# Dilated heads in 64x64 score blocks: one turning for two heads, fewer stores, later loads, and a head of attention in another order

## The chip, the cores and the metric

The kernel runs on one core of one Trainium2 chip. The metric is the device time of one execution in microseconds, smaller is better. Three runs of the kernel before gave a median of 2364.34 us (2364.12 to 2364.73).

## The reference, cut to what matters

Two layers. Each normalises x, projects it to q, k and v, mixes tokens in three groups of heads, projects back, and adds a SwiGLU feed-forward part. All arithmetic is float32. The change touches group C, six heads of dilated attention. Each head attends in three branches, with dilation 1, 4 and 16 (in the code: `mid` tiles, `c2` and `c3`), and the branches are merged by their softmax denominators.

```python
DIL_BRANCHES = ((128, 1), (512, 4), (2048, 16))

def dilated_attention(q, k, v, slopes):
    b, h, s, hd = q.shape
    outs, lses = [], []
    for window, d in DIL_BRANCHES:
        L = s // d                     # 1024, 256, 64
        def to_sub(t):                 # every d-th token: d subsequences of L tokens
            return t.reshape(b, h, L, d, hd).transpose(0, 3, 1, 2, 4).reshape(b * d, h, L, hd)
        o, lse = banded_attention(to_sub(q)[:, :, None], to_sub(k), to_sub(v),
                                  window // (2 * d), slopes[:, None], d)
        ...
    w = jax.nn.softmax(jnp.stack(lses), axis=0)
    o = jnp.einsum("nbhs,nbhsd->bhsd", w, jnp.stack(outs).astype(jnp.float32))
```

With dilation 16 a subsequence (a remainder of the position by 16) has 64 tokens, and each of its tokens attends to those 64. With dilation 4 it has 256 tokens, and a block of 128 queries needs 192 keys.

## The kernel before

**Stages of a layer.** Values and 14 units of 128 q/k columns are projected (`half_unit`, 24 matmuls per half unit), normalised over each head by ACT (`qk_square`, `qk_rms`, `qk_variance`) and DVE (`square_low`, `qk_finish`), then come attention, the output projection and the feed-forward part. Outside attention every product is three matmuls 512 columns wide.

**Tiles and steps of attention.** A tile is one head against one block of 128 queries. `tiles` has 48 tiles of kind `c3` (dilation 16), 48 of `c2` (dilation 4), and 128 of the banded kinds `b0`, `mid`, `b7`. Four tiles make a step: steps 0 to 11 score `c3`, 12 to 23 `c2`, 24 to 55 the rest. Six dilated tiles (the six heads) make a group `gi`, 0 to 15, a step and a half each. In a step k, `pe_step(k)` does in this order

- the scores of tiles 4k to 4k+3 (`score_pair`, two pairs),
- the products with the values of tiles 4k-8 to 4k-5 (`weigh`),
- the turning of the weights of tiles 4k-4 to 4k-1 (`unit`: transposes into PSUM).

DVE adds the distance table to the scores and takes the minimum (`tmin`), ACT takes the exponential (`exponential`), and the turned weights are copied from PSUM to `PT` by DVE or ACT (`copy_unit`; DVE's copy is the last thing in its step, and with one row of a step DVE has it). `weigh` in step k+1 waits for the copies of step k (`copied`). Tile n keeps its weights in `T[:, n % 8, :]`.

**c3 before.** One tile takes two remainders at once: 128 queries against 128 keys. The two 64x64 blocks off the diagonal are masked out by the table (1e34). A tile has one turning of 128 columns, `weigh` does two matmuls for it, one for each 64 queries. **c2 before.** 128 queries against 192 keys, two turnings (the second one of columns 128 to 255, its last 64 unused), four matmuls in `weigh`. A step of four tiles turns 4 blocks of 128 columns in `c3`, 8 in `c2`; they lie in one or two rows of up to 512 columns, each copied by one instruction.

**POOL.** `stage(gi)` gathers queries and keys of group gi from `QK` into `QS`, `KS` (two buffers; it waits until group gi-2 is scored, and `score_pair` waits for it). Between the stages POOL clears parts of `VC` (gi 4) and `VR` (gi 5), takes the power of the last unit's variances (gi 7, `POWERED`), and multiplies that unit by the roots (`scale_last(0)`, `scale_last(1)`, gi 12 and 13), which step 24 needs (`qk_s`). After stage 15 it makes the 12 tables of the grid heads (`bias_table`), which step 27 needs.

**SP's one queue.** For each gi, in order: `store_group(gi)` (waits until ACT has put the group away, `grp_s`), perhaps `spread_roots` (the variances go out to DRAM and come back transposed, their roots go out and come back broadcast to 64 partitions; its last step writes `RM_LAST`, which `scale_last` waits for), `load_values(gi + 4)`, then other loads for later: `MASK`, `BIAS`, `VC` (`load_neighbours`), `VA` (`load_grid`). After gi 15 come the stored groups of the first banded block (`g_back`), which `branch_min(0)` on DVE waits for in step 27.

**The head of attention.** The score of tile 0 comes after the last product of unit 13. DVE does tile 0's `tmin` and then `square_low(13, 1)`. ACT does `qk_square(13, 1)`, `qk_variance(26)`, `keep_raw(0)` and then the first exponential; in step 1 also `qk_variance(27)` and `keep_raw(1)`.

```python
                sp.wait_ge(stat, 2 * QT)          # before the first load_values
...
                    elif gi in (12, 13):
                        scale_last(gi - 12)
...
                for gi in range(C_GROUPS):
                    store_group(gi)
                    if gi in SPREAD_AT:
                        spread_roots(SPREAD_AT[gi])
                    if gi + 4 < C_GROUPS:
                        load_values(gi + 4)
```

## Time and profile before

| what | value |
|---|---|
| median of 3 runs | 2364.34 us |
| profiled execution, its own time | 2367.3 us |
| its span, first to last instruction | 2365.8 us |
| mean granted TensorE clock | 0.996 of full |
| busy share of the span: PE, DVE, ACT, POOL | 99%, 67%, 45%, 28% |
| steps 0 to 24 of attention, layer 0 | 255.88 to 316.60 us |
| the same, layer 1 | 1430.35 to 1490.97 us |

The span is cut in engines' busy times, in stretches, and in single instructions with the idle time ahead of them and what ended it. A float32 matmul of attention appears as two records (8 records are 4 matmuls), a transpose as one. A record's length includes its way through the array, so records overlap; the price of one more is the distance between starts, not the length. The last half unit of the projection and the two dilated kinds together take some 61 us in each layer.

### The profile page before, as it was taken

The numbers are of one execution on the slowest core, as the hardware profiler recorded it, in microseconds if no ns is written. First come the engines' busy times: TensorE is split into PE (matmuls) and PEld (weight loads), VectorE is DVE, ScalarE is ACT, GpSimd is POOL, SyncE is SP. The second block draws the span as 40 slices with busy tenths as digits, with TensorE's granted clock in tenths as the row PEclk, the third lists the DMA queues.
The fourth block names the chain that finished last, engine by engine and source line by source line (L and its number), as shares of the span: only waits on it lengthen the run. The fifth ranks groups of instructions, "written<-read, shape, count | busy, mean of one in ns | idle before, by whom it ended". The sixth has DMA issues, their size and how long they took to land. (4 is left out here: it accounts for less than half of the span.)

```text
span 2365.8 us, 38274 instructions
## 1 busy us (share of the span) xinstructions
PE 2330.3 (99%) x14504; PEld 1933.6 (82%) x14504; DVE 1592.7 (67%) x2871; ACT 1073.1 (45%) x2048; POOL 656.5 (28%) x571
## 2 busy tenths in 40 slices
PE   9999999999999999999999999999999999999998
PEld 9988777787888888888898887777878888888887
DVE  5389778737555555789844897787475555557897
ACT  4333778735223222444533338786452222324434
POOL 1000456411544444100010005553124444441000
PEclk9999999999999999999999999999999999999999
DMA  6231341231222211721352214303322222218222
GB/s 236 68 58 53 88 123 30 76 135 66 91 84 80 87 57 54 292 77 63 111 187 57 55 44 133 86 23 122 107 71 81 81 80 81 58 49 311 71 81 98
DMA packets 233986, 225.19 MB, mean 95 GB/s; under 512 B 50260, under 2 KB 192084, under 8 KB 233816
## 3 DMA queue, kind: packets, MB, share of 16 engines
q1 hardware_dynamic: 233816, 222.89, 29.5%
q8 instruction: 110, 1.80, 0.3%
q14 instruction: 60, 0.49, 0.1%
HBM read 171.00 MB, written 53.41 MB: 95 GB/s over the span
## 5 line engine op out<-in xcount | busy, mean ns | idle before, releaser
L1810 DVE TENSOR_TENSOR WL<-RAW,WH 128x512 fp32r<-128x512 f32 x132 | 160.5, 1217 | 151.3 <-ACT WH L1276 151.3
L2506 PE MATMUL psum<-ABH 128*128 128x512 f32 x616 | 240.1, 390 | 1.1 <-DVE X L1896 1.1
L2507 PE MATMUL psum<-ABL,ABH 128*128 128x512 f32 x616 | 239.7, 389 | 0.0
L2508 PE MATMUL psum<-ABH,ABL 128*128 128x512 f32 x616 | 239.7, 389 | 0.0
L2472 PE MATMUL psum<-HL,WH 128*128 128x512 f32 x704 | 217.4, 390 | 0.7 <-DVE HL L1816 0.7
L2472 PE MATMUL psum<-OPH_t,WH 128*128 128x512 f32 x528 | 207.1, 392 | 5.9 <-DVE U L1831 5.9
L2472 PE MATMUL psum<-OPL_t,WH 128*128 128x512 f32 x528 | 207.1, 392 | 1.0 <-DVE OPH_t L1816 1.0
L1810 DVE TENSOR_TENSOR WL<-WS,WH 128x512 fp32r<-128x512 f32 x172 | 138.5, 806 | 84.2 <-ACT WH L1276 84.2
L2151 POOL TENSOR_TENSOR WS<-RAW 128x512 f32<-128x512 f32 x84 | 143.3, 1706 | 130.6 <-DMA x_res<-X 130.6
L2183 PE MATMUL psum<-HH,UH 128*128 128x512 f32 x448 | 174.6, 390 | 1.3 <-ACT VB L1050 1.3
L2184 PE MATMUL psum<-HL,UH 128*128 128x512 f32 x448 | 174.3, 389 | 0.0
L2185 PE MATMUL psum<-HH,UL 128*128 128x512 f32 x448 | 174.3, 389 | 0.0
L1500 DVE RECIPROCAL RM<-RM 128x512 f32<-128x512 f32 x52 | 174.0, 3345 | 0.0
L1126 ACT ACTIVATE T<-T,G 128x192 f32<-128x192 f32 (+3 forms) x352 | 154.0, 468 | 28.8 <-DVE G L1547 26.6
L2472 PEld LDWEIGHTS psum<-HL,WH 128*128 128x128 f32 x704 | 131.7, 188 | 29.2 <-DVE HL L1816 1.5
L2048 POOL COPY QS<-QK 128x384 f32<-128x384 f32 x32 | 30.2, 943 | 443.6 <-DVE QK L1503 255.8
L2183 PE MATMUL psum<-PH,HH 128*128 128x512 f32 (+1 forms) x384 | 143.7, 374 | 0.0
L2185 PE MATMUL psum<-PH,HL 128*128 128x512 f32 (+1 forms) x384 | 142.6, 371 | 0.0
L2184 PE MATMUL psum<-PL,HH 128*128 128x512 f32 (+1 forms) x384 | 142.5, 371 | 0.0
L2472 PE MATMUL psum<-OPH_t,WL 128*128 128x512 f32 x352 | 138.2, 393 | 0.0
L2506 PEld LDWEIGHTS psum<-ABH 128*128 128x128 f32 x616 | 115.6, 188 | 26.8 <-DVE X L1896 2.0
L2472 PE MATMUL psum<-OPH_b,WH 128*128 128x512 f32 x352 | 137.1, 390 | 0.0
(262 smaller groups left out, 5587.7 us busy)
## 6 DMA issues: line engine op xcount, KB each, us to landing
RAW<-in_w_gu SPq DMA_DIRECT2D x176, 256.0 KB, 3.9
WDS<-in_w_down SPq DMA_DIRECT2D x88, 256.0 KB, 2.5
UR<-in_w_in SPq DMA_DIRECT2D x56, 256.0 KB, 3.3
g_mid<-GRES SPq DMA_DIRECT2D x28, 512.0 KB, 2.6
WDK<-in_w_down SPq DMA_DIRECT2D x44, 256.0 KB, 5.9
x_res<-X SPq DMA_DIRECT2D x2, 4096.0 KB, 13.0
PR<-in_w_out SPq DMA_DIRECT2D x32, 256.0 KB, 4.8
X<-x_res SPq DMA_DIRECT2D x2, 4096.0 KB, 13.0
```

What stands on the lines that cost most here:

```text
L1126: a.activation(T[:, n % 8, off:off + w], T[:, n % 8, off:off + w], ACT.Exp, scale=-1.0, bias=G[:, 6 * V1 + place_:6 * V1 + place_ + 1]).th ...
L1500: v.reciprocal(RM[:, hf, :], RM[:, hf, :]).then_inc(rec_s, 1)
L1810: v.tensor_tensor(WL[SLOT[i, j]][:, :, :], w_source(i, j), WH[SLOT[i, j]][:, :, :].bitcast(F32), ALU.subtract).then_inc(w_lo, 1)
L2048: g.tensor_copy(dst, dilated_rows(bd, T_CQ, q, P)).then_inc(staged, 1)
L2151: g.tensor_tensor(to[i][:, :, :], first, second, op).then_inc(w_sum, 1)
L2183: t.matmul(dst, sh, mh, start=start, stop=False)
L2184: t.matmul(dst, sh, ml, start=False, stop=False)
L2185: return t.matmul(dst, sl, mh, start=False, stop=stop)
L2472: last = t.matmul(dst[:, :], w[SLOT[i, j]][:, k, :], h[o][:, k, :], start=(i in (1, 5, 6) and k == 0 and part == 0), stop=(i in (2, 3, 4) ...
L2506: t.matmul(dst, ah, bh, start=open_, stop=False, skip_group_check=True)
L2507: t.matmul(dst, ah, bl, start=False, stop=False, skip_group_check=True)
L2508: last = t.matmul(dst, al, bh, start=False, stop=shut, skip_group_check=True)
```

## The change

1. **c3 scores.** `score_pair` does two 64x64 matmuls per tile instead of one of 128x128: each half of the output partitions holds one remainder's 64 keys. Scores, table, `tmin` and exponential are 64 columns wide. The two heads of a pair write their weights side by side in `T` (`weights_of`), and one turning of 128 columns does both. The values `VR` hold the even heads on partitions 0 to 63 and the odd ones on 64 to 127, zeros elsewhere, so that `weigh` (`products_of`) still does two matmuls per tile.
2. **c2.** Two heads' 192 columns lie side by side: three turnings per pair instead of four. Rows are 384 columns instead of 512; in `c3` the one row is 256. `weigh` keeps four matmuls per tile.
3. **Layout.** `v_c` and `VC` have the heads in another order (even, then odd). Loads of `VR`: two per group in `c3` (pieces of 780 B), three instead of two in `c2`. Stores of a `c3` group: one DMA instead of two. `VR` is cleared at gi 1 by two memsets, instead of at gi 5 by one.
4. **Moves.** `spread_roots(2)` and `(3)` go from gi 6 and 7 to 9 and 11, POOL's power from gi 7 to 9, `scale_last` from gi 12 and 13 to 14 and 15. `MASK` from 7 to 8; `BIAS` from one each at 8 to 11 to gi 8, 10, 10, 12; `VC` from 8 to 12 to gi 12 and 13; `VA` from two each at 12 to 15 to four each at 14 and 15. ACT makes a `TC2` table every second step, `TC1` in steps 12 to 17, `TB` in 18 to 23.
5. **Head.** The scores of tiles 0 and 1 are put inside the last half unit, after its fifth k. DVE's `square_low(13, 1)` comes after the fourth tile. ACT does `keep_raw(0)`, then `qk_square(13, 1)`, then the exponentials; `qk_variance(26)` comes after the fourth of them, `keep_raw(1)` and `qk_variance(27)` after the eighth. The slot of tile n in `T` is (n + 6) % 8.

```diff
-            SPREAD_AT = {0: 0, 1: 1, 6: 2, 7: 3}
+            SPREAD_AT = {0: 0, 1: 1, 9: 2, 11: 3}
...
-                if k == "c3":
-                    return [0]
-                if k == "c2" or k in ("b0", "b7") or 6 <= s < 12:
+                if dilated(bd):
+                    return [] if s % 2 else [0] if k == "c3" else [0, 128, 256]
+                if k in ("b0", "b7") or 6 <= s < 12:
                     return [0, 128]
...
-                        i = (k - 1) % 2 if need == 1 else len(rows) % 2
+                        i = max(k - 2, 0) % 2 if need == 1 else len(rows) % 2
...
+            def weights_of(n):
+                bd, s = tiles[n]
+                w, off = width(bd, s)
+                if dilated(bd):
+                    pair_, at_ = n - n % 2, n % 2 * w
+                    return T[:, t_slot(pair_), at_:at_ + w]
+                return T[:, t_slot(n), off:off + w]
...
+            def products_of(n):
+                bd, s = tiles[n]
+                odd, h, q = s % 2, s % 6 // 2, s // 6
+                own = slice((3 * odd + h) * V1, (3 * odd + h + 1) * V1)
+                if bd["kind"] == "c3":
+                    return [(place_of[n - odd, 0], VR[:, q, rr, own], (64 * rr,)) for rr in range(2)]
+                if bd["kind"] == "c2":
+                    return [(place_of[n - odd, 256 * odd], VR[:, q, 0, own], (0, 64)),
+                            (place_of[n - odd, 128], VR[:, q, 1, own], (0, 64))]
...
-                sp.wait_ge(stat, 2 * QT)
+                sp.wait_ge(scored, 2)
...
-                        for rr in range(2):
-                            sp.dma_start(g16[2 * gi + rr], G4[64 * rr:64 * rr + 64, slot, :]).then_inc(g_out_s[slot], 16)
+                        sp.dma_start(g16[2 * gi:2 * gi + 2], G4[:, slot, :]).then_inc(g_out_s[slot], 16)
...
-                    if gi == 7:
+                    if gi == 8:
                         sp.dma_start(MASK[:, :], masks).then_inc(mask_in, 16)
-                    elif 8 <= gi < 8 + A_H:
-                        h = gi - 8
-                        load_neighbours(2 * h)
-                        load_neighbours(2 * h + 1)
-                        sp.dma_start(BIAS[:, h, :], biases[:, 384 * h:384 * h + 384]).then_inc(rpb_in, 16)
-                    elif gi >= C_GROUPS - COLS // 2:
...
+                        load_bias(0)
+                    elif gi == 10:
+                        load_bias(1)
+                        load_bias(2)
+                    elif gi == 12:
+                        load_bias(3)
+                        for m in range(4):
+                            load_neighbours(m)
+                    elif gi == 13:
+                        for m in range(4, MT + 1):
+                            load_neighbours(m)
+                    elif gi >= C_GROUPS - 2:
+                        for c in range(COLS // 2):
+                            load_grid(COLS // 2 * (gi - (C_GROUPS - 2)) + c)
...
                 keep_raw(0)
-                act.wait_ge(stat, 2 * QT)
+                qk_square(QT - 1, 1, 1)
                 for k in range(GROUPS + 1):
                     act_step(k)
...
-                        if (k, j) == (0, 0):
+                        if (k, j) == (0, 1):
+                            dve.wait_ge(sq_lo, 2 * QT - 1)
+                        elif (k, j) == (0, 3):
                             square_low(QT - 1, 1)
                             dve.wait_ge(sq_lo, 2 * QT)
+                            dve.wait_ge(qk_s, 2 * QT - 2)
...
-                    if gi == 4:
+                    if gi == 1:
                         pool.wait_ge(stat, 2 * QT)
+                        pool.wait_ge(staged, 4)
+                        for hh in range(2):
+                            others = slice(64 - 64 * hh, 128 - 64 * hh)
+                            g.memset(VR[others, :, :, 3 * V1 * hh:3 * V1 * hh + 3 * V1], 0.0).then_inc(v_ones, 1)
+                            pool.wait_ge(v_ones, 3 + hh)
...
-                    elif gi == 7:
+                    elif gi == 9:
                         pool.wait_ge(root_s, SPREAD_IN)
...
-                    elif gi in (12, 13):
-                        scale_last(gi - 12)
+                    elif gi in (14, 15):
+                        scale_last(gi - 14)
...
+                FIRST_SCORES = 4
+                def score_pair(n, free):
+                    bd, s = tiles[n]
+                    if dilated(bd) and s % 6 == 0:
+                        pe.wait_ge(staged, 2 * (bd["G"] + s // 6 + 1))
...
+                    if bd["kind"] == "c3":
+                        for rr in range(2):
+                            own = slice(64 * rr, 64 * rr + 64)
+                            for h in range(2):
+                                last = t.matmul(scores(n + h)[own, :], queries(bd, s + h)[:, own], keys(bd, s + h)[:, own],
+                                                start=True, stop=True)
+                                if rr:
+                                    last.then_inc(scored, 1)
+                        return
...
+                        if isinstance(u, int) and (u, hf, k) == (QT - 1, 1, FIRST_SCORES):
+                            score_pair(0, lambda: pe.wait_ge(qk_s, 2 * QT - 3))
```

## Rows read from the trace of the kernel before

**Rows 1.** The page, busy time (share of the span) and instructions.

```profile
PE 2330.3 (99%) x14504; PEld 1933.6 (82%) x14504; DVE 1592.7 (67%) x2871; ACT 1073.1 (45%) x2048; POOL 656.5 (28%) x571
```

**Rows 2.** Busy time by engine from 284 to 312 us, mostly c2 steps.

```profile
284.00:312.00 28.00, 27.66 (x442) 23.10 (x441) 17.29 (x89) 24.26 (x62) 15.83 (x15) 1.00 0.85 236
```

**Rows 3.** Timeline, a c3 step: start, length, engine, line, records, idle before.

```profile
274.69 0.55 PEld L2322 LDWEIGHTS psum<-VR,PT 128*64 128x64 f32 x16 [0.33 <-DVE PT L1718]
...
275.31 0.66 PE L2296 MATMUL psum<-ident,T 128*128 128x128 f32 x4
...
275.89 0.72 PE L2283 MATMUL psum<-KS,QS 64*128 64x128 f32 x8
```

**Rows 4.** Timeline, a c2 step, PE and DVE.

```profile
297.15 0.35 DVE L1547 CUSTOM_DVE_ANT_0 T<-TC,psum 128x192 f32<-128x192 f32 x1
...
297.83 1.09 PE L2296 MATMUL psum<-ident,T 128*128 128x128 f32 x8
...
298.96 0.69 DVE L1718 COPY PT<-psum 128x512 f32<-128x512 f32 x1 [1.17 <-PE psum L2296]
...
299.70 1.15 PE L2322 MATMUL psum<-VR,PT 128*64 128x65 f32 x32
```

**Rows 5.** Timeline of PE, layer 0: turnings of steps 3, 12, 14, 23 and 25.

```profile
265.02 0.66 PE L2296 MATMUL psum<-ident,T 128*128 128x128 f32 x4
...
283.53 0.65 PE L2296 MATMUL psum<-ident,T 128*128 128x128 f32 x4
...
288.96 1.09 PE L2296 MATMUL psum<-ident,T 128*128 128x128 f32 x8
...
315.57 1.09 PE L2296 MATMUL psum<-ident,T 128*128 128x128 f32 x8
...
322.32 1.09 PE L2296 MATMUL psum<-ident,T 128*128 128x128 f32 x8
```

**Rows 6.** Timeline of the head of attention in layer 0, ACT and PE.

```profile
255.34 0.60 ACT L1067 ACTIVATE SQ<-psum 128x512 f32<-128x512 f32 x1 [2.54 <-PE psum L2185]
...
256.51 0.67 ACT L1080 ACTIVATE RM_LAST<-psum,eps 128x512 f32<-128x512 f32 x1
...
257.08 1.11 ACT L1108 ACTIVATE QK<-psum,GAINS 128x512 f32<-128x512 f32 x1
...
257.84 1.00 PE L2283 MATMUL psum<-KS,QS 64*128 64x128 f32 x8 [1.24 <-DVE G L1547]
...
257.99 0.36 ACT L1126 ACTIVATE T<-T,G 128x128 f32<-128x128 f32 x1
```

**Rows 7.** Two stretches at that place; the number before the last two is the granted clock.

```profile
257.00:258.00 1.00, 0.16 (x2) 0.16 (x4) 0.96 (x6) 1.00 (x3) 0.00 (x0) 1.00 0.48 131
...
259.00:263.00 4.00, 3.82 (x31) 2.74 (x31) 2.02 (x13) 4.00 (x12) 2.05 (x4) 0.58 0.39 110
```

**Rows 8.** Timeline of POOL, layer 0: power, product with the roots, a c2 stage, last table.

```profile
276.26 2.93 POOL L2100 TENSOR_TENSOR ROOTS<-ROOTS,neghalf 128x16 f32<-128x16 f32 x1
...
295.73 1.54 POOL L2069 TENSOR_TENSOR QK<-QK,RM_LAST 128x512 f32<-128x512 f32 x1
297.21 0.91 POOL L2048 COPY QS<-QK 128x384 f32<-128x384 f32 x1
298.07 1.23 POOL L2049 COPY KS<-QK 128x576 f32<-128x576 f32 x1
...
320.69 1.01 POOL L2062 TENSOR_TENSOR TA<-MASK,BIAS 128x384 f32<-128x384 f32 x1
```

**Rows 9.** Timeline of SP's queue, layer 0: roots back, store of group 10.

```profile
290.11 1.24 SPq L849 DMA_DIRECT2D RM_LAST<-variances  x2
...
301.51 0.32 SPq L861 DMA_DIRECT2D g_d<-G  x1
```

**Rows 10.** DMAs issued from 289 to 297 us: size, median us to landing.

```profile
g_d<-G SPq DMA_DIRECT2D x2, 99.0 KB, 2.3
...
BIAS<-biases SPq DMA_DIRECT2D x1, 192.0 KB, 5.5
```

More of the change, by code:

```diff
@@ L532, in width @@
                 if k == "c3":
-                    return 128, 0
+                    return 64, 0
                 if k == "c2":
@@ L1544, in tmin @@
                     if k == "b0" and s in (6, 12):
-                        dve.wait_ge(g_out_s[0 if s == 6 else 3], 96)
+                        dve.wait_ge(g_out_s[0 if s == 6 else 3], 64)
                     acc = G[:, 6 * V1 + place_:6 * V1 + place_ + 1]
-                    v.tensor_tensor_reduce(out=T[:, n % 8, off:off + w], in0=table(bd, s), in1=scores(n),
+                    v.tensor_tensor_reduce(out=weights_of(n), in0=table(bd, s), in1=scores(n),
                                            scale=1.0, scalar=3.0e38, op0=ALU.add, op1=ALU.min,
@@ L2234, in _ @@
                             ins.then_inc(moved, 1)
+                FIRST_SCORES = 4
[3 more added lines that the diff above has]
+                        pe.wait_ge(staged, 2 * (bd["G"] + s // 6 + 1))
+                    if n == 4 * first_group(0):
+                        pe.wait_ge(qk_s, 2 * QT)
+                    free()
+                    if bd["kind"] == "c3":
+                        for rr in range(2):
+                            own = slice(64 * rr, 64 * rr + 64)
[5 more added lines that the diff above has]
+                        return
+                    for h in range(2):
+                        t.matmul(scores(n + h), queries(bd, s + h), keys(bd, s + h), start=True,
+                                 stop=True).then_inc(scored, 1)
                 def half_unit(u, slot, hf, dst, hb=None):
@@ L2271, in _ @@
                 qk_unit_steps(QT - 1, 1)
-                def score_pair(n, free):
-                    bd, s = tiles[n]
-                    if dilated(bd) and s % 6 == 0:
-                        pe.wait_ge(staged, 2 * (bd["G"] + s // 6 + 1))
-                    if n == 4 * first_group(0):
-                        pe.wait_ge(qk_s, 2 * QT)
-                    free()
-                    for h in range(2):
-                        t.matmul(scores(n + h), queries(bd, s + h), keys(bd, s + h), start=True,
-                                 stop=True).then_inc(scored, 1)
                 def unit(u):
                     if u["y"] is None:
-                        pe.wait_ge(exp_s, u["items"][-1][0] + 1)
-                        srcs = [T[:, n % 8, c:c + P] for n, c in u["items"]]
+                        n_last = u["items"][-1][0]
+                        pe.wait_ge(exp_s, n_last + (2 if dilated(tiles[n_last][0]) else 1))
+                        srcs = [turned_cols(n, c) for n, c in u["items"]]
                     else:
@@ L2318, in weigh @@
                     place_ = group_buf(bd, s)[1]
-                    for c, col in enumerate(chs):
-                        u, i = place_of[n, col]
-                        for q0 in (0, 64):
+                    opened = set()
+                    for c, ((u, i), v_, halves) in enumerate(parts):
+                        for q0 in halves:
+                            shut = not any(q0 in part[2] for part in parts[c + 1:])
                             last = t.matmul(group_bank(bd, s)[q0:q0 + 64, place_ * V1:place_ * V1 + V1],
-                                            PT[:, u["slot"], P * i + q0:P * i + q0 + 64], values(bd, s, c),
-                                            start=(c == 0), stop=(c == len(chs) - 1))
+                                            PT[:, u["slot"], P * i + q0:P * i + q0 + 64], v_,
+                                            start=q0 not in opened, stop=shut)
+                            opened.add(q0)
                     last.then_inc(pv_s, 1)
```

113 lines of the change are left out of this document (60 added, 53 removed).

## The prediction

> **What bounds the kernel now.** I read the page first: PE is busy 99% of the span, the next engine 67% [rows 1]. So only what shortens PE's own sequence, or a hole in it, counts, and the change touches that sequence only from the last half unit to step 25, in both layers alike. Of that stretch I read the busy times [rows 2]: ACT is at 24.3 of 28 us there, near enough to PE to have to be checked. Then came the timeline, where one c3 step shows what sets the pace. PE's weight loads for `weigh` wait 0.33 us for DVE's copy of the turned weights [rows 3]. The ring is: four turnings (0.66 us to the last one's end), 0.03, DVE's copy of 512 columns (0.69, as in rows 4), 0.06, `weigh` until the next turning (275.31 - 274.69 = 0.62). That is 2.06 us, and nine steps took (283.53 - 265.02) / 9 = 2.057 [rows 5]. In c2 the ring is 1.09 + 0.04 + 0.69 + 0.05 + some 1.08 = 2.95, and nine steps took (315.57 - 288.96) / 9 = 2.957 [rows 4, 5]. The scores lie beside the copy and are nearly hidden. The reader is to see a ring of PE and DVE in which PE has only 0.33 us to spare.
>
> Below, t(k) is the start of step k's turnings. I work in layer 0 and count twice.
>
> **Head.** Before, ACT begins the last squares at 255.34, and 1.17 us later the variance, then `keep_raw(0)`, and only at 257.99 the first exponential; PE stands 1.24 us before its next scores [rows 6]. After, `keep_raw(0)` lies ahead of the last squares, in ACT's wait of 2.54 us [rows 6]. The squares start some 0.45 us later, because scores are squeezed into the half unit (eight records of 128 columns take 0.53 us, see c3 steps; here they have 64). First exponential at 255.34 + 0.45 + 1.2 = 257.0. ACT then has, up to tile 11's exponential, twelve exponentials, two variances (0.67), `keep_raw(1)` (1.11) and one table. An exponential of 64 columns I take at 0.24 us from start to start, against 0.36 long for 128 [rows 6]: 2.9 + 1.3 + 1.1 + 0.3 = 5.6 us, which gives t(3) = 262.6 against 265.02 [rows 5]. **Head: -2.4 us**, -1.0 if each exponential takes 0.36, -3.0 if the variances overlap their neighbours. In this I count the clock as full. Before, the hole (PE busy 0.16 us of 1) was followed by 3.4 us at 1.2 GHz: 4 us at a mean of 0.58 [rows 7]. The new head has only holes of under 0.4 us.
>
> The new wait of POOL (two memsets at gi 1, then stage 2) ends about where stage 2 did, because stage 2 waited for the scores of step 1 anyway; I cost it at nothing, hidden by the tiles of stages 0 and 1, which last until step 3. It costs what it is late if steps 0 to 2 are faster than I say.
>
> **c3 steps.** The ring now has two turnings and a copy of 256 columns. Turnings: four end after 0.66, eight after 1.09, so 0.107 apiece, and two end after 0.44. The copy: 192 columns of `tmin` take 0.35 and 512 of a copy 0.69 [rows 4], so about 1.06 ns per column, and 0.69 - 0.27 = 0.42 (bounds 0.35, half, and 0.69). Ring: 0.44 + 0.03 + 0.42 + 0.06 + 0.62 = 1.57. PE's own work was 2.057 - 0.33 = 1.73; less two turnings (0.2) it is 1.53 if sixteen short score records cost what eight did: 0.53, since the scores of the step shown began at 275.89 - 2.06 = 273.83, and PE was free for `weigh` at 274.69 - 0.33 = 274.36. The nearest row for a record of 64 weight columns and about 64 moving ones is `weigh`: sixteen weight loads in 0.55 us [rows 3], 0.034 each. The other bound is the old price, 0.53 / 8 = 0.066 each, 1.06 us. I take the nearest row: the ring sets 1.57 (PE's work is 1.55), and a step saves 0.49. Steps 3 to 13 are ten: **-4.9 us**. ACT's four exponentials fall, and its table comes every second step, so it keeps up.
>
> The Trainium skill has a rule against this (TensorEngine Tiling, Performance Considerations, Instruction Overhead): a matmul carries an overhead of about 60 cycles, and a free dimension of 1 takes as long as one of 60. If that came on top of 64 columns, an estimate from the page is 124 cycles at 2.4 GHz, 0.052 us a record, and a c3 step of about 1.83 us. The `weigh` records here, at 0.034 us, speak against such a sum.
>
> A faster c3 brings the stores forward: slot 0 of `G4` is wanted again at step 6. By the order of ACT's step its store is issued some 1.2 us after t(3), takes SP 0.6 and lands 2.3 later [rows 10], at t(3) + 4.1; `tmin` wants it at t(3) + 3.5. The next three queue behind roots and loads on SP. **+0.8**, between 0 (one store instead of two) and 1.5.
>
> **c2 steps.** Six turnings end after 0.87, the copy of 384 columns takes 0.69 - 0.135 = 0.555: ring 2.957 - 0.22 - 0.135 = 2.60. PE's work falls by 0.2 too. ACT is busy 24.3 of 28 us, 2.57 a step [rows 2]; its copy is shorter by 0.13 too, so it fits into 2.60, with little to spare. A step saves 0.35; steps 13 to 25 are twelve: **-4.2 us**. Together so far -10.7 us per layer.
>
> **What is moved past what.** POOL's power (2.93 us) now lies between stages 9 and 10 [rows 8]. Stage 10 is wanted in step 15, four steps after the scores that stage 9 waits for; two stages of 2.1 and the power are 7.1 of the some 8 us. At nothing, 0.5 if late.
>
> The roots are another matter. `spread_roots(3)` now stands behind `store_group(11)`, so it waits until ACT has put group 11 away in step 19. For group 10 that was at 301.51 [rows 9], with t(18) = 288.96 + 4 x 2.957 = 300.79 [rows 5]: 0.72 after the turnings began. So: store at t(19) + 0.7, then the two `RM_LAST` DMAs, 0.62 of SP each, the second begun at t(19) + 1.7. A DMA there took between 2.3 and 5.5 us to land [rows 10]; I take the middle, 4.0: t(19) + 5.7. On POOL `scale_last(0)` waits for that, and behind it in POOL's order is stage 15, which PE wants for the second pair of step 22. From rows 8: 1.48 for the product, 2.06 for the stage, done at t(19) + 9.25. Then PE scores the pair and does its `weigh` (0.45 + 1.1): t(22) = t(19) + 10.8. Without the wait it were 3 x 2.60 = 7.8. **+3.0 us**, between 1.3 (landing 2.3) and 4.5 (landing 5.5). Before, the same DMAs were issued at 290.11 and used at 295.73, so this wait was nobody's.
>
> That hole is longer than the 1.24 us one of the head, behind which the clock fell to 1.2 GHz for 3.4 us [rows 6, 7]. In c2 PE works nearly all the time (27.66 of 28 us busy before [rows 2]), so half of 3.4 is lost, less what falls into the hole itself: **+1.3**, between 0 and 1.7. The Trainium skill (TensorE: Matmul & The Clock Gate, Part 1) says that the gate passes every second pulse after idleness until PE has been busy again for a while. By that rule it happens; the head of this trace agrees (0.58 over 4 us behind the hole).
>
> `scale_last(1)` now precedes the grid tables; they ended at 321.70 [rows 8] with step 27 beginning at about t(25) + 4.6 = 326.9. After, they start some 5 us later against t(22), and still end before step 27, because the wait at stage 15 has moved step 27 too. At nothing; up to 2 if that wait were absent from PE but present on POOL, which it can't be. The loads of `VA` are bunched: two more of some 0.6 us lie ahead of `g_back`, which DVE wants in step 27: **+0.3**, between 0 and 1.2. The other loads land steps ahead.
>
> **Sum.** -2.4 - 4.9 + 0.8 - 4.2 + 3.0 + 1.3 + 0.3 = -6.1 us per layer, -12.2 in all. The span 2365.8 becomes 2353.6, the profiled execution 2367.3 becomes 2355.1. The median of the runs is 3.0 under that execution: 2364.3 - 12.2 = 2352.1 us.
>
> **Rivals.**
> - *Roots in time.* The DMAs land in 2 us or less and PE hides the rest, or POOL is quicker: no hole and no fall of the clock. -10.4 per layer, 2343.5. For it: group 11's traffic is light beside that of rows 10. Against: even 2.3 leaves 1.3 us. Chance 0.17.
> - *Short records at full price.* Sixteen at 0.066 us make PE's work 2.06 in c3, and ten steps save nothing, nor are stores late: +4.1, 2360.3; by something between, such as 1.83 a step, 2356 or so. Against: the `weigh` rows. Chance 0.15.
> - *Slower, by the roots.* If `RM_LAST` arrives late enough, the chain SP, POOL, PE eats all. Without that wait and the clock the change brings 10.4 us per layer; the wait costs 3.0 at a landing of 4.0, so with the clock's 1.3 it turns at a landing of 4.0 + 6.1 = 10.1 us. At 13 us the time is 2370. Nothing in rows 10 is above 5.5. Chance 0.04.
> - *Moved, not won.* The ring is shorter, but ACT or the `staged` and store waits hold c3 and c2 near the old pace, and only the head is gained against the new hole: -2.4 + 3.0 and nothing else, 2365. For it: ACT at 24.3 of 28 [rows 2]. Against: its work falls too. Chance 0.08.
> - *The forecast*, with its bounds: 2347 to 2357. Chance 0.56.
>
> **Range and chances.** 2343 to 2359 leaves out the last two rivals and part of the full price. A measurement of this kernel tells some 0.2% (4.7 us) from no change. Faster by more: 0.86 (forecast, roots in time, most of the full price); within: 0.09; slower: 0.05.
>
> **What would show it.** c3 turnings 1.57 us apart, c2 2.60; copies of 0.42 and 0.555; t(3) some 2.4 us nearer to the last unit; the granted clock full in steps 0 to 3; in step 22 PE waiting for POOL's `KS` some 3 us behind `scale_last(0)`, which waits for a DMA, and the clock at 0.5 after it. Wrong would be: PE's scores in c3 longer than 0.55, DVE waiting for `g_d` all along c3, or no idle PE in step 22.

## The result, and the profile after

Median 2405.4 us (2404.2 to 2406.7, four runs) against 2364.5 us (2364.1 to 2365.9, four runs): the ratio is 1.0169, with a 95% interval of 1.0157 to 1.0181. The change makes the kernel 41 us slower, and the forecast of 2352.1 was wrong in sign. The profiled execution took 2406.65 us, its span is 2404.5 us and the mean granted clock 0.985 (0.996 before).

The page of the changed kernel, busy time by engine, to be held against [rows 1]:

```profile
PE 2331.5 (97%) x14600; PEld 1929.9 (80%) x14600; DVE 1579.9 (66%) x2871; ACT 1063.6 (44%) x2048; POOL 659.5 (27%) x573
```

PE is busy for as long as before (2331.5 and 2330.3 us), though it has fewer columns to do; the span is 38.7 longer. So the time went into idle PE, and into work at a lower clock that ate what the shorter steps save. Where, the starts of the turnings show (from the timelines of PE, layer 0; the last two kernels are experiments, below):

| step | before | after | `flat_only` | `flat_spread` |
|---|---|---|---|---|
| 3 | 265.02 | 261.68 | 261.29 | 261.54 |
| 6 | 271.19 | 266.43 | 266.04 | 266.30 |
| 14 | 288.96 | 298.88 | 282.55 | 283.54 |
| 21 | 309.66 | 319.98 | 301.73 | 302.72 |
| 22 | 312.62 | 330.55 | 312.11 | 305.46 |
| 27 | 329.58 | 347.52 | 328.95 | 321.64 |
| 28 | 333.48 | 353.21 | 336.20 | 325.87 |

After minus before: -3.3 us at step 3, -4.8 at step 6, then +14.7 from 6 to 14, +0.4 from 14 to 21, +7.6 from 21 to 22, nothing from 22 to 27, +1.8 from 27 to 28. That is +19.7 by step 28 of layer 0. Step 28 of layer 1 begins 38.2 us later than before (1546.08 and 1507.85), so these places hold nearly all of the 38.7 between the spans.

Of the 3.3 us at step 3, 0.8 isn't the head's. The first squares of the layer, which no edit moves, already start that much earlier in this trace (ACT, before, then after):

```profile
96.65 0.60 ACT L1067 ACTIVATE SQ<-psum 128x512 f32<-128x512 f32 x1 [4.67 <-PE psum L2185]
```

```profile
95.87 0.60 ACT L1112 ACTIVATE SQ<-psum 128x512 f32<-128x512 f32 x1 [5.00 <-PE psum L2230]
```

**The head** went as forecast. ACT after, timeline, where [rows 6] stood:

```profile
255.06 0.60 ACT L1112 ACTIVATE SQ<-psum 128x512 f32<-128x512 f32 x1 [2.01 <-PE psum L2230]
...
256.23 1.05 ACT L1167 ACTIVATE T<-T,G 128x64 f32<-128x64 f32 x4
257.18 0.67 ACT L1125 ACTIVATE RM_LAST<-psum,eps 128x512 f32<-128x512 f32 x1
```

Exponentials begin at 256.23 instead of 257.99 (0.8 us of it from further back, as said), four of 64 columns take 1.05 us, 0.26 each, and the variance comes behind them.

**The short steps** went as forecast too, while nothing disturbed them. PE, steps 5 to 7:

```profile
264.86 0.44 PE L2355 MATMUL psum<-ident,T 128*128 128x128 f32 x2
265.23 0.46 PE L2295 MATMUL psum<-KS,QS 64*64 64x64 f32 x16
265.81 0.69 PE L2382 MATMUL psum<-VR,PT 128*64 128x65 f32 x16
266.43 0.44 PE L2355 MATMUL psum<-ident,T 128*128 128x128 f32 x2
270.78 0.87 PE L2295 MATMUL psum<-KS,QS 64*64 64x64 f32 x16 [3.91 <-DVE G L1587]
```

From turning to turning it is 1.57 us. Its weight loads, in the same place:

```profile
265.22 0.32 PEld L2295 LDWEIGHTS psum<-KS,QS 64*64 64x64 f32 x16 [0.17 <-issue]
265.81 0.55 PEld L2382 LDWEIGHTS psum<-VR,PT 128*64 128x64 f32 x16 [0.26 <-DVE PT L1758]
```

Sixteen short score records have their loads done in 0.32 us, and `weigh` still waits 0.26 us for the copy: the ring is the forecast's. Then, in step 7, PE stands 3.91 us for DVE, and the next scores take 0.87 instead of 0.46, at a granted clock of 0.50 (271 to 272 us). Whom DVE waits for, and with it everyone, the waits of 250 to 345 us say (waited for; us in total, times, longest):

```profile
DVE T L1587 <- DMA g_d<-G: 20.0, 7, 4.3
...
POOL QK L2112 <- DMA RM_LAST<-variances: 8.8, 1, 8.8
...
PE psum L2301 <- POOL KS L2092: 6.3, 1, 6.3
```

The first was 0.2 us in that stretch before. The timelines put the stores on SP's queue (the two numbers are when an issue starts and how long it has SP) beside the minima that wait for them on DVE:

```profile
263.02 0.61 SPq L895 DMA_DIRECT2D g_d<-G  x1
...
265.76 0.54 SPq L895 DMA_DIRECT2D g_d<-G  x1
...
271.95 0.53 SPq L895 DMA_DIRECT2D g_d<-G  x1
```

```profile
270.01 0.22 DVE L1587 CUSTOM_DVE_ANT_0 T<-TC,psum 128x64 f32<-128x64 f32 x1 [4.25 <-DMA g_d<-G]
275.27 0.22 DVE L1587 CUSTOM_DVE_ANT_0 T<-TC,psum 128x64 f32<-128x64 f32 x1 [3.58 <-DMA g_d<-G]
280.55 0.22 DVE L1587 CUSTOM_DVE_ANT_0 T<-TC,psum 128x64 f32<-128x64 f32 x1 [2.22 <-DMA g_d<-G]
```

Store 0 is issued at 263.02 and DVE goes on at 270.0: 7.0 us. By the same reckoning, from issue to use, store 1 takes 9.5 us and store 2 8.6. A store of half that size landed after 2.3 us before [rows 10]. The DMA view of 276.2 to 283 us shows why; the first line is the busy share of the 16 DMA engines in 40 slices, in tenths, the second what they moved:

```profile
DMA  2111111111117782378411111101111111111111
GB/s 65 37 56 37 47 37 37 56 47 37 47 37 129 207 276 79 83 180 276 143 46 41 41 42 51 56 37 56 56 37 47 47 47 47 47 47 47 47 37 56
```

Whenever a store is alone under way, the share is a tenth, which is about two engines of 16, and the rate some 45 GB/s (37 to 56). When loads run, it is seven or eight tenths and up to 276 GB/s. The store is narrow, not large.

The granted clock, in four stretches (the third number from the end):

```profile
259.00:263.00 4.00, 3.22 (x75) 2.23 (x72) 2.02 (x19) 4.00 (x13) 2.77 (x4) 1.00 0.09 23
268.00:272.00 4.00, 1.22 (x24) 1.02 (x26) 1.42 (x13) 1.59 (x6) 0.66 (x1) 0.86 0.16 54
272.00:278.00 6.00, 4.06 (x58) 2.85 (x58) 1.45 (x14) 2.67 (x10) 2.56 (x4) 0.50 0.37 106
278.00:290.00 12.00, 9.31 (x118) 6.87 (x116) 3.47 (x28) 4.45 (x16) 5.57 (x5) 0.50 0.35 100
```

In the head, where it was 0.58 [rows 7], it is now full. Behind the holes of the stores it is 0.50, the level of 1.2 GHz, and it stays there to 290 us, with a new hole in every group.

**Step 22** has the chain of the forecast. SP, POOL and PE:

```profile
315.49 1.06 SPq L915 DMA_DIRECT2D BIAS<-biases  x2
316.60 0.43 SPq L898 DMA_DIRECT2D g_d<-G  x1
317.07 1.09 SPq L887 DMA_DIRECT2D RM_LAST<-variances  x2
```

```profile
324.18 1.53 POOL L2112 TENSOR_TENSOR QK<-QK,RM_LAST 128x512 f32<-128x512 f32 x1 [8.80 <-DMA RM_LAST<-variances]
...
326.43 1.20 POOL L2092 COPY KS<-QK 128x576 f32<-128x576 f32 x1
```

```profile
327.68 1.01 PE L2301 MATMUL psum<-KS,QS 64*128 64x192 f32 x4 [6.30 <-POOL KS L2092]
330.55 1.54 PE L2355 MATMUL psum<-ident,T 128*128 128x128 f32 x6
```

The roots leave SP at 317.07 and POOL has them at 324.18. Six turnings, 0.88 us long otherwise, take 1.54 in this step: the granted clock is 0.50 from 328 to 332 us, behind the hole.

**Step 28** shows the last loss: DVE's minimum over the stored groups waits, and PE for it.

```profile
349.96 0.17 DVE L1674 TENSOR_TENSOR nmin<-G 128x6 f32<-128x6 f32 x1 [2.97 <-DMA G<-g_d]
```

### The profile page after: what moved, and what is told of

Read it like the earlier page. It is cut to its first block and busy times, and to the rows that moved or that the text cites. A ratio compares the mean times of both kernels' runs of the same rounds, so it can differ in the third digit from the quotient of the medians.

```text
span 2404.5 us, 38460 instructions
## 1 busy us (share of the span) xinstructions
PE 2331.5 (97%) x14600; PEld 1929.9 (80%) x14600; DVE 1579.9 (66%) x2871; ACT 1063.6 (44%) x2048; POOL 659.5 (27%) x573
## 5 line engine op out<-in xcount | busy, mean ns | idle before, releaser
L1167 ACT ACTIVATE T<-T,G 128x192 f32<-128x192 f32 (+3 forms) x352 | 148.6, 455 | 75.2 <-DVE G L1587 73.5
L2536 PE MATMUL psum<-OPH_b,WL 128*128 128x512 f32 x352 | 137.0, 389 | 0.0
```

The lines of the kernel that those rows point to most:

```text
L1167: a.activation(weights_of(n), weights_of(n), ACT.Exp, scale=-1.0, bias=G[:, 6 * V1 + place_:6 * V1 + place_ + 1]).then_inc(exp_s, 1)
L2536: last = t.matmul(dst[:, :], w[SLOT[i, j]][:, k, :], h[o][:, k, :], start=(i in (1, 5, 6) and k == 0 and part == 0), stop=(i in (2, 3, 4) ...
```

## The experiments

The kernel before was timed beside each set, so ratios are compared, not times.

**1. Is it the form of the store?** Two kernels from the changed one, and one from the kernel before. The one store of the change runs over 2 remainders, 64 rows of each and 396 columns; its outermost dimension is the 2. Each of the two old stores runs over 64 rows and 396 columns, so there it is 64. `two_stores` cuts the store by remainder, as it was:

```diff
-    sp.dma_start(g16[2 * gi:2 * gi + 2], G4[:, slot, :]).then_inc(g_out_s[slot], 16)
+    for rr in range(2):
+        sp.dma_start(g16[2 * gi + rr], G4[64 * rr:64 * rr + 64, slot, :]).then_inc(g_out_s[slot], 16)
```

> The kernel after, with the store of a c3 group as two DMAs again, one for each remainder (each 64 rows of 1584 B); all else as after. Theory A (the one DMA, whose outermost dimension is the two remainders, is carried by about 2 of the 16 DMA engines): in the trace after it ran at some 50 GB/s, and DVE stood 20 us in layer 0 waiting for it. With two DMAs it should land in 2 to 3 us as before, DVE's waits for the stores should go to under 2 us, the c3 steps should come every 1.6 us, the clock should stay full there, and the turnings of steps 6 to 14 should be some 15.5 us apart instead of 32.5: -17 us per layer, 2371 us in all (2366 to 2376). The hole at stage 15 (10.6 us from step 21's turnings to step 22's) and DVE's 3 us wait in step 27 should stay. Theory B (the stores are slow because the value loads in 780 B pieces and SP's queue crowd the engines): nothing or little changes, 2400 to 2406.

`col_halves` cuts it by columns instead, so that each half is small but has the same outermost dimension of 2:

```diff
-    sp.dma_start(g16[2 * gi:2 * gi + 2], G4[:, slot, :]).then_inc(g_out_s[slot], 16)
+    for cc in range(2):
+        sp.dma_start(g16[2 * gi:2 * gi + 2, :, 198 * cc:198 * cc + 198],
+                     G4[:, slot, 198 * cc:198 * cc + 198]).then_inc(g_out_s[slot], 16)
```

> As two_stores, but the two DMAs of a c3 group each carry half of the columns of both remainders (2 x 64 pieces of 792 B), so the size and the number of DMAs are those of two_stores while the outermost dimension stays 2. Theory A (engines by the outermost dimension): still about 2 engines busy, still 4 us or more of transfer per DMA, and DVE waits as after or longer: 2403 to 2430. Theory C (one DMA of 198 KB is too big or comes too late to the queue, two of half the size spread better): 2366 to 2380, like two_stores.

`before_one_store` is the kernel before with the changed kernel's store and nothing else (the first diff, the other way round). In all of them the counts that the waits for stores use follow the number of DMAs.

> The kernel before with only the store of a c3 group made one DMA of both remainders, the form of the change; nothing else. Theory A: the store takes the time that it took after, DVE's first tile of each group from step 6 on waits for it, and c3 steps slow down from 2.06 us to about 3.4 us each on average, with spells of half clock: +10 to +15 us per layer, 2385 to 2394. Theory B (pieces of 780 B and a faster c3 are what made it late, not the form of the store): same as before, 2364 to 2368.

| kernel | median us | ratio | 95% interval | DVE's waits for `g_d`, layer 0 |
|---|---|---|---|---|
| two_stores | 2377.5 | 1.0046 | 1.0029 to 1.0063 | 5.3 us |
| col_halves | 2417.2 | 1.0219 | 1.0201 to 1.0236 | 24.6 us |
| before_one_store | 2392.4 | 1.0114 | 1.0098 to 1.0131 | 15.2 us |

The store of two 64-row DMAs takes off 29 us (1.0169 to 1.0046). Two DMAs that are half as large but have an outermost dimension of 2 take off nothing; they add 12. And the store alone makes the kernel before 26 us slower (2392.4 against 2366.1). Size and number are out, the form is in. `two_stores` came out 6 us above the 2371 expected, and above its range: DVE still waits 5.3 us for stores. SP's queue shows where:

```profile
266.59 1.24 SPq L896 DMA_DIRECT2D g_d<-G  x2
267.88 0.60 SPq L880 DMA_DIRECT2D ROOTS<-variances  x1
268.53 1.28 SPq L858 DMA_DIRECT2D VR<-v_c  x2
269.85 1.24 SPq L896 DMA_DIRECT2D g_d<-G  x2
```

Two stores and two loads are 2.52 us of issues, and a group of c3 now lasts a step and a half, 2.36 us. Thus the faster steps run into the queue, even with the old stores.

**2. The late roots.** `roots_back` is the changed kernel with the roots in their old places:

```diff
-            SPREAD_AT = {0: 0, 1: 1, 9: 2, 11: 3}
+            SPREAD_AT = {0: 0, 1: 1, 6: 2, 7: 3}
...
-                    if gi == 9:            # POOL's power
+                    if gi == 7:
...
-                    elif gi in (14, 15):
-                        scale_last(gi - 14)
+                    elif gi in (12, 13):
+                        scale_last(gi - 12)
```

> The kernel after, with the roots at their places of before (spread_roots at gi 6 and 7, POOL's power at gi 7, scale_last at gi 12 and 13). Theory A (scale_last(0) waits for RM_LAST, stage 15 is queued behind it on POOL, PE waits for stage 15): the hole of 6.3 us in step 22 goes, step 22's turnings come 2.8 us after step 21's instead of 10.6, and the slow clock behind it (3.4 us at half) goes too: -7.6 to -8.5 us per layer, 2389 us (2386 to 2392). Theory B (the hole is the late loads and stores on the shared queue, whatever POOL waits for): it stays or moves, 2400 to 2406.

2393.5 us, ratio 1.0115 (1.0098 to 1.0132): 12.8 us less than the changed kernel by the ratios, and 1.5 us above the expected range. Steps 21 and 22 are 2.75 us apart (319.50, 322.25), so the hole is gone. Part of the gain is lost again at step 28: steps 27 and 28 are 7.65 us apart (338.42, 346.07) instead of 5.69. PE's wait there is 2.51 us instead of 1.90, and behind it the granted clock is 0.50 (342 to 345 us), where the changed kernel kept 1.00; its next eight score records take 2.93 us instead of 1.69. The growth is thus mostly the clock.

**3. Everything on SP's queue back, and the two halves of that.** `two_back` has the two stores and the roots back; `three_back` has the loads of `MASK`, `BIAS`, `VC` and `VA` in their old places as well; `three_back_old_head` also has the old order of the head.

> The kernel after with three things as before: two store DMAs per c3 group, the roots' places, and the places of the loads (MASK, BIAS, VC, VA). The tiles, the turnings and the head stay those of the change. Theory A (the loss is these three, the rest of the change wins): in two_stores the turnings of step 21 began at 304.4 us against 309.7 before, and what followed lost it; with the hole at stage 15 and DVE's 3.1 us wait for g_back in step 27 gone, each layer keeps 5.5 to 6 us: 11 to 12 us under the kernel before, ratio 0.9953 (0.994 to 0.997). Rival (something in the new tiles costs in the banded steps too, or the holes only move): within 0.2% of before or slower.

> As three_back, but the loads stay where the change put them (VC at gi 12 and 13, VA four each at 14 and 15, BIAS later). Theory A (the bunched VA loads stand ahead of g_back on SP's queue and on the DMA engines, and branch_min(0) in step 27 waits 3 us for it, PE loses 1.8 to 2.5): slower than three_back by 1.8 to 3 us per layer, 3.6 to 6 us in all, and DVE's nmin waits some 3 us for a DMA. Rival (that wait came from the late roots or the slow stores upstream): within 1 us of three_back, no such wait.

> As three_back, with the head of attention as before too: scores of tile 0 after the last product, ACT with squares, variance and keep_raw before the first exponential, the first value loads after the last product. Theory A: the head brings 3.3 us per layer (turnings of step 3 at 261.5 instead of 265.0, and no fall of the clock), of which the waits for stores take some back: 2.5 to 3.4 us per layer slower than three_back, 5 to 7 us in all; the clock falls to half behind a hole of over 1 us in steps 0 to 3. Rival (what the head wins is lost again at the first stores of c3, which only wait longer): within 2 us of three_back.

| kernel | median us | ratio | 95% interval |
|---|---|---|---|
| two_back | 2363.1 | 0.9987 | 0.9978 to 0.9996 |
| three_back | 2360.4 | 0.9980 | 0.9969 to 0.9991 |
| three_back_old_head | 2363.6 | 0.9991 | 0.9982 to 1.0000 |

`three_back` missed its expectation by 6 us (0.9953 expected) and lies where its rival put it, within 0.2% of the kernel before: DVE still waits 10.2 us for stores in layer 0, in ten places. Six of them are in c2 (5.1 us), where SP has seven issues for each of the groups 8 to 11: a store, three of `VR`, two of `VC` and one of `BIAS`. The places of the loads are worth some 2 us, which the intervals don't separate; 3.6 to 6 were expected. In `two_back` PE waits 1.7 us at step 28 and the step takes 5.45 us; with the loads back it takes 3.90, as before. So the bunched loads cause that wait, and what they gain in c2 (6.8 us of waits for stores instead of 10.2) offsets part of it.

The old head costs 2.6 us by the ratios (0.9980 and 0.9991, whose intervals overlap), where 5 to 7 were expected. The turnings show that the head's gain isn't eaten further on, it is that small beside the new tiles: step 3 begins at 262.82 with the old head and at 261.33 with the new one, 1.5 us for the layer. In `before_flat` (below), with old tiles and old head, it begins at 263.60, and the first squares of the layer start within 0.05 us of each other in all three traces. The forecast's 2.4 us of head are thus 0.8 from narrower tiles and 1.5 from the new order.

**4. One store, and wide.** `flat_store` is `three_back` with the scratch of that branch kept remainder by remainder, so that a group is 128 rows in a line and one DMA with an outermost dimension of 128 writes it; the load in step 27 gathers it instead.

```diff
-    g16 = g_dil[1].rearrange("(j r) c -> r j c", r=16)
-    for rr in range(2):
-        sp.dma_start(g16[2 * gi + rr], G4[64 * rr:64 * rr + 64, slot, :]).then_inc(g_out_s[slot], 16)
+    sp.dma_start(g_dil[1][P * gi:P * gi + P, :], G4[:, slot, :]).then_inc(g_out_s[slot], 16)
...
-    sp.dma_start(GC[:, 1 + n, :], g_dil[n][b * P:b * P + P, :]).then_inc(g_back, 16)
+    src = g_dil[1].rearrange("(r j) c -> j r c", r=16)[8 * b:8 * b + 8] if n else g_dil[0][b * P:b * P + P, :]
+    sp.dma_start(GC[:, 1 + n, :], src).then_inc(g_back, 16)
```

> As three_back, but with one store DMA of 198 KB per c3 group whose outermost dimension is 128 on both sides: the scratch tensor of the third branch is kept remainder by remainder, so that a group's rows are contiguous, and the load back of a block has the reordering instead (outermost dimension 8). Theory A (the outermost dimension sets how many engines carry a DMA; its size or the single DMA does not): the store lands in some 3 us, SP's queue has three issues per c3 group instead of four, DVE's waits for stores (5.3 us in layer 0 of two_stores) fall to under 3 us: 1 to 3 us per layer faster than three_back, ratio 0.993. Theory C (one DMA of 198 KB in c3 is slow by itself): DVE waits 15 us or more per layer for the stores, 2385 or more. A risk: the load back on 8 engines comes late in step 27, +1 to 2 us.

2353.7 us, ratio 0.9951 (0.9937 to 0.9964): faster than both kernels. DVE still waits 5.6 us for stores in layer 0, where under 3 were expected. The same 198 KB now land after 3.4 us (median of the DMAs issued from 266 to 271 us):

```profile
g_d<-G SPq DMA_DIRECT2D x2, 198.0 KB, 3.4
```

`before_flat` is the kernel before with that store and nothing else.

> The kernel before with one store per c3 group, as in before_one_store, but contiguous in DRAM so that its outermost dimension is 128, with the load back reordered. Theory A (only the outermost dimension of 2 made before_one_store 28 us slower): the same as the kernel before, 2363 to 2368, since its c3 steps hardly waited for a store (0.2 us in all). Theory C (one DMA per group is worse than two by its size): 2375 or more.

2364.5 us, ratio 0.9997 (0.9988 to 1.0006): no difference. One DMA of 198 KB in the slower old steps costs nothing if it is wide, and costs 26 us if its outermost dimension is 2. The wide store also writes its rows in one piece of DRAM, where the narrow one strides; that the form matters without this is shown by `two_stores` and `col_halves`, which keep the addresses.

**5. Thinning SP's queue.** `flat_tuned` is `flat_store` with the loads spread evenly over groups 8 to 15 and the first roots two groups later; `flat_spread` has the even loads alone.

```diff
-            SPREAD_AT = {0: 0, 1: 1, 6: 2, 7: 3}
+            SPREAD_AT = {2: 0, 3: 1, 6: 2, 7: 3}      # flat_tuned alone
...
+                    if 8 <= gi < 12:
+                        load_bias(gi - 8)
+                    for m in {9: (0,), 10: (1, 2), 11: (3, 4), 12: (5, 6), 13: (7, 8)}.get(gi, ()):
+                        load_neighbours(m)
+                    for c in {11: (0,), 12: (1, 2), 13: (3, 4), 14: (5, 6), 15: (7,)}.get(gi, ()):
+                        load_grid(c)
```

> flat_store (one contiguous store per c3 group, roots at gi 6 and 7), with the first two parts of the roots moved from gi 0 and 1 to gi 2 and 3, behind the stores that DVE waited for first, and the loads of BIAS, VC and VA spread evenly over gi 8 to 15 with only one VA load at gi 15. Theory A (what remains in flat_store is SP's queue in steps 5 to 12 and in c2: DVE waited 2.6 us for stores in c3 and 3.0 in c2, layer 0): waits fall by a third to a half, 0.5 to 1.5 us per layer, 2351 to 2353. Rival (the pow on POOL at gi 7 now waits for the roots, stage 8 comes late): 2354 to 2358.

2360.5 us, ratio 0.9975 (0.9965 to 0.9985). The loads were spread, yet the time rose, above even the 2354 to 2358 of the rival. Layer 1, POOL and PE:

```profile
1441.91 2.92 POOL L2137 TENSOR_TENSOR ROOTS<-ROOTS,neghalf 128x16 f32<-128x16 f32 x1 [2.30 <-DMA ROOTS<-variances]
...
1446.93 0.92 PE L2293 MATMUL psum<-KS,QS 64*128 64x192 f32 x8 [3.09 <-POOL KS L2084]
```

POOL's power waits for the first parts of the roots, which now come two groups later; stage 8 stands behind it, and PE waits 3.09 us for that stage. Whether that alone was it, the last pair tells.

> flat_store with its loads spread evenly over groups 8 to 15, as in flat_tuned, but the first two spread_roots left at groups 0 and 1. flat_tuned was 6.8 us slower than flat_store, and its trace showed POOL waiting for the roots (2.3 us at the power) and PE for POOL's KS at stage 8 (1.8 and 3.1 us). Theory: that late spread alone spoiled flat_tuned. Then stage 8 is in time, DVE's waits for stores in c2 are at most 0.5 us per layer against some 3 in flat_store, and the ratio to before is 0.9940 (0.9930 to 0.9951), 2350 to 2354 us. Rival: the spread loads themselves collide with the stores or come late for their users. Then the ratio stays near flat_tuned's, 0.9965 to 0.9980, with no wait of PE for KS at stage 8.

2352.7 us, ratio 0.9947 (0.9933 to 0.9960): equal to `flat_store` within the intervals, and PE doesn't wait for stage 8. The late first parts of the roots alone had spoiled `flat_tuned`. In layer 0 of `flat_spread` three waits for stores are left, all in c3 (3.4 us; `flat_store` had 5.6), the largest of them this one:

```profile
272.89 0.22 DVE L1579 CUSTOM_DVE_ANT_0 T<-TC,psum 128x64 f32<-128x64 f32 x1 [2.33 <-DMA g_d<-G]
```

**6. The changed kernel with nothing but a wide store.** `flat_only` has the diff of experiment 4 and no other.

> The changed kernel with nothing undone but the form of the c3 store (one 198 KB DMA of 128 rows, the scratch kept remainder by remainder). Roots and loads stand where the change puts them. Theory: the stores cost some 30 us, the late roots 12 to 14 and the bunched loads some 3, and they add up. Then flat_store's 0.9951 plus 14 and 3 us gives a ratio of 1.0023 (1.0005 to 1.0035), about 2370 us, with PE's wait for POOL's KS at step 22 still 5 to 6 us in each layer. Rival: the hole at step 22 was long because the stores had crowded SP's queue and the DMAs; with the stores quick RM_LAST lands in about 4 us, the hole is near the 3.0 us of the prediction, and the ratio is 0.998 or less.

2372.2 us, ratio 1.0029 (1.0019 to 1.0039); 1.0023 was expected from adding the parts. PE's wait in step 22 is as long as with the narrow stores (waits of 250 to 345 us):

```profile
PE psum L2301 <- POOL KS L2092: 6.1, 1, 6.1
```

So the rival falls by which the crowd of slow stores had made the roots late. The parts add up to within 1.5 us of what was expected. In this order, the narrow store costs 33 us (1.0169 - 1.0029), the later roots and bunched loads 18 us (1.0029 - 0.9951), and what remains of the change gains 12 (0.9951). The sizes depend on the order: the store alone cost the kernel before 26 us. With the stores wide, the change as designed is still 0.3% slower than the kernel before, and the whole interval of `flat_only` lies above 1.

## Why the prediction was wrong, point by point

**The step that failed: the term for the stores that a faster c3 brings forward, +0.8 with bounds 0 and 1.5.** It read "one store instead of two" as at worst harmless (it is the reason for the bound 0) and took the landing of 2.3 us from [rows 10]. That row is of DMAs of another form, with 64 or 128 rows outermost. The new one has the two remainders outermost on the DRAM side, so about two engines carry 198 KB (a share of one tenth), and its first use comes 7.0 to 9.5 us after the issue. Steps 6 to 14 took 32.4 us; without any wait they would have taken some 14.6 (six steps of 1.57, one of 1.84, one of 3.3, the last two from `flat_only`). So the term was 17.8 us per layer, idle time and the slow clock behind it together, and not 0.8. Experiments 1, 4 and 6 show it from four sides. The store is also wanted much more than once: the text costed slot 0 at step 6 and gave the next three no price, but a late store makes its slot late for every group, and DVE waited seven times.

This could have been read from the diff. The Trainium skill (DMA: Bandwidth & Descriptors, in "Why a DMA increments its semaphore by 16 and not by 1", and again under "Rules for kernel authors") says that the number of engines for a DMA from SP is the largest k up to 16 that divides the slowest non-1 dimension of both sides; for `g16[2 * gi:2 * gi + 2]` that gives 2. The trace agrees: a share of one tenth, some 45 GB/s.

**Head, -2.4 forecast:** right. Step 3 begins 3.3 us earlier, and without the 0.8 us from ahead of attention it is 2.6, within the bounds. The clock stayed full as forecast. Set against the layer's first squares, the last squares start 0.5 us later (0.45 forecast), and the first exponential, at 256.23, is where the forecast's 257.0 less 0.8 puts it.

**c3 steps, 1.57 forecast:** 1.57 where undisturbed, with the copy at 0.42, both to the hundredth. The choice of the nearest row for short score records was right: sixteen take 0.32 us of weight loads, 0.020 each against the 0.034 taken. The rival "short records at full price" (1.06) is refuted, and so is the estimate worked out from the Trainium skill (TensorEngine Tiling, Performance Considerations, Instruction Overhead), 0.052 us a record and 1.83 us a step. But the -4.9 of ten steps was never reached: in layer 0 `flat_spread` gains 1.6 us from step 3 to step 12 of the 4.4 that nine steps are worth. The missing 2.8 fall in the steps where DVE waits for stores (3.4 us in all): steps 8 to 10 take 5.39 us (269.67 to 275.06) instead of 3.14.

**c2 steps, 2.60 forecast:** mis-sized. Steps 17 to 21 of the changed kernel are 2.74 apart (309.02 to 319.98), so a step saves 0.22 and not 0.35. One of them, PE, its weight loads and DVE:

```profile
314.50 0.88 PE L2355 MATMUL psum<-ident,T 128*128 128x128 f32 x6
315.30 0.63 PEld L2301 LDWEIGHTS psum<-KS,QS 64*128 64x128 f32 x8 [0.17 <-issue]
...
315.41 0.56 DVE L1758 COPY PT<-psum 128x384 f32<-128x384 f32 x1 [0.99 <-PE psum L2355]
315.47 0.47 ACT L1184 ACTIVATE PT<-psum 128x384 f32<-128x384 f32 x1
316.15 1.01 PEld L2382 LDWEIGHTS psum<-VR,PT 128*64 128x64 f32 x32 [0.22 <-ACT PT L1184]
```

The same place before:

```profile
301.81 0.63 PEld L2283 LDWEIGHTS psum<-KS,QS 64*128 64x128 f32 x8 [0.17 <-issue]
...
301.92 0.69 DVE L1718 COPY PT<-psum 128x512 f32<-128x512 f32 x1 [1.17 <-PE psum L2296]
302.66 1.01 PEld L2322 LDWEIGHTS psum<-VR,PT 128*64 128x64 f32 x32 [0.23 <-issue]
```

`weigh` starts 0.85 us after the scores did, in the new step and in the old one alike, although the new copies end at 315.97 and 315.94, 0.2 us before it. It isn't the copy that paces the new c2, but PE's own sequence, so only the two turnings less (0.22) count. `flat_only` and `flat_spread` have the same 2.74 us a step, but no run changed the copy alone. The forecast's ring had closed to 0.01 us for the old steps, where the copy ended 0.05 before `weigh`: two paths of one length, and it took both to be shorter.

**Roots, +3.0 and clock +1.3:** right mechanism, too small; +7.6 measured between steps 21 and 22. Against step 19 (turnings at 314.50) the store was issued at +2.1 instead of +0.7, since two `BIAS` loads of 0.53 us each stood on SP ahead of it (315.49), which the working had passed over. The landing took 7.1 us from the first issue and 6.6 from the second, against 4.0. So POOL had the roots at +9.7, not +5.7, and PE scored at +13.2, not +9.25. From there to the turnings it was 2.87 us instead of 1.55: that is the 1.3 of the clock. The landing isn't the store's doing: in `flat_only`, with wide stores, it was 6.9 us from the first issue (298.84 to 305.74). What the DMA view adds is the traffic. From 317 to 324.3 us the 16 engines were 97% busy with 1.7 MB, of which the roots are two DMAs of 256 KB and the rest mostly loads of `BIAS`, `VR` and `VC`; in `flat_only` it is 95% and the same amount. The prediction had called group 11's traffic light. No run moved these loads away from late roots, so how much of the 7 us they make isn't shown.

**`g_back`, +0.3 with bounds 0 and 1.2:** +1.8 in step 28 of layer 0 here, beyond the outer bound, and +3.35 in `flat_only` (7.25 us instead of 3.90). The term had no clock in it. In `flat_only` PE waits 2.55 us instead of 1.90 and the granted clock then falls (0.58 from 335 to 338 us); the rest is that.

**The rivals.** None of them was what happened. "Slower, by the roots" had the right sign and the wrong place; its turning point, a landing of 10.1 us, was not reached (6.6 from the second issue, as the forecast counts). Even so `flat_only`, which has no narrow store, is slower than the kernel before: steps 21 and 22 are 7.4 us further apart there than before, for the landing, the later issue and the clock together, and the change without them gives less than the 10.4 counted on. "Moved, not won" names waits for stores, at no worse than 2365. The end of the text named the real one as a mark of failure, "DVE waiting for `g_d` all along c3", without giving it a chance or a price. "Roots in time" is what the change is without the mistakes: 2343.5 forecast, 2352.7 measured in `flat_spread`. By the ratio that is 2351.8 against the median of 2364.3 that the forecast started from. By the spans (2365.8 and 2350.6) 15.2 of the forecast's 20.8 us were gained. Of the 5.6 missing, the mis-sized c2 saving is 3.1 (twelve steps of 0.13, twice), and the store waits of c3 are 2.9 beyond the 0.8 a layer that the forecast had for them (2.8 lost in layer 0, 1.7 in layer 1); the head gives a little back. The rest of the 8 us isn't the change's: the profiled execution before lay 3 us above its median, the one of `flat_spread` on its own.

## What to carry to other kernels

Before two DMAs are made one, look at the outermost dimension of both sides, not at the bytes: a loop over 2 that becomes a dimension of 2 puts the whole transfer on two engines, where 128 rows outermost are as quick as the pair. A landing taken from the trace is good only for a DMA of the same form and in like traffic. When a loop gets faster, the issues in it (here 2.5 us on SP for a group of 2.36) are the next bound to add up. And if a step's ring (the round of waits that sets its pace) closes exactly, see whether a second path of the same length exists before you shorten the first.

## What the runs showed of the hardware that was not expected

- The same 198 KB are there 7.0 to 9.5 us after the issue with an outermost dimension of 2, and in 3.4 with 128; a kernel with two DMAs of 99 KB with 2 outermost was slower still (ratio 1.0219).
- The weight loads of sixteen score records of 64 by 64 take 0.32 us, 0.020 each, where eight of 128 columns took 0.52, 0.065 each: half the columns, under a third of the price.
- With holes of 2 to 4 us in every group, the granted clock stayed at 0.50 from 272 to 278 us and from 278 to 290, where PE was busy 4.06 of 6 and 9.31 of 12 us. A single hole can go either way, and not by its length alone: behind PE's wait of 1.90 us at step 28 the clock stayed at 1.00 in the changed kernel (350.5 to 354 us), though it had fallen behind the 1.24 us of the old head, and behind the 2.51 us of `roots_back` it fell to 0.50.
